# Five feed-forward parts on one core: a fourth pair of chunks as seven block products, all third and fourth block sums by accumulating transfers, and a new order of the units

## What is computed

```python
def swiglu(h, w_in, w_out):
    gate, up = jnp.split(h @ w_in, 2, axis=-1)
    return (jax.nn.silu(gate) * up) @ w_out      # first network: h 256 x 1024, hidden width 2816

def _swiglu(x, wg, wu, wd):                      # second network, four times
    return (jax.nn.silu(x @ wg) * (x @ wu)) @ wd

h = _swiglu(_rmsnorm(x, g[0]), ffn_w_gate[l, 0], ffn_w_up[l, 0], ffn_w_down[l, 0])
x = x + 0.5 * _rmsnorm(h, g[1])
```

## Time and profile before

| | before |
|---|---|
| median of three runs | 1266.3 us (1266.28 to 1269.35) |
| the profiled execution, its own time | 1265.96 us |
| its span, first to last instruction | 1264.2 us |
| TensorE busy | 1246.7 us (99%) |
| VectorE busy | 986.2 us (78%) |
| ScalarE busy | 757.5 us (60%) |
| GpSimd busy | 103.3 us (8%) |
| granted TensorE clock, mean | 0.999 |

### The profile page before, as it was taken

One profiled execution on the slowest core, in us unless ns is written; L12 is line 12 of the kernel. 1 busy time (PEld: TensorE's weight loads), 2 busy tenths in 40 slices (PEclk: granted clock), 3 DMA queues, 4 the chain that ended last, 5 costly groups with the idle time before them and its releaser, 6 DMA issues. The chain is left out here.

```text
span 1264.2 us, 16581 instructions
## 1 busy us (share of the span) xinstructions
PE 1246.7 (99%) x6615; PEld 1021.0 (81%) x6615; DVE 986.2 (78%) x1005; ACT 757.5 (60%) x929; POOL 103.3 (8%) x133
## 2 busy tenths in 40 slices
PE   8999999999999999999999999999999999999998
PEld 6887788887788888877888887888888897788886
DVE  4487788997898896676877986977976687888895
ACT  5344556565655665657665667565767555755663
POOL 3000000000554000100000000000000200000000
PEclk9999999999999999999999999999999999999999
DMA  9997499774598555662797565986763543598562
GB/s 335 370 401 248 136 351 282 265 208 157 169 327 283 200 150 200 204 182 69 268 292 236 171 183 165 338 261 183 214 209 109 184 137 131 196 306 263 200 176 75
DMA packets 150098, 279.23 MB, mean 221 GB/s; under 512 B 9800, under 2 KB 82820, under 8 KB 146820
## 3 DMA queue, kind: packets, MB, share of 16 engines
q1 hardware_dynamic: 143360, 243.28, 56.0%
q0 software_dynamic: 6288, 34.69, 12.0%
q10 hardware_dynamic: 372, 0.19, 0.1%
HBM read 248.73 MB, written 1.05 MB: 198 GB/s over the span
## 5 line engine op out<-in xcount | busy, mean ns | idle before, releaser
L2048 DVE TENSOR_TENSOR w_lo<-raw,w_hi 128x2048 fp32r<-128x2048 f32 x135 | 309.6, 2300 | 74.0 <-ACT w_hi L1476 73.6
L1476 ACT ACTIVATE w_hi<-raw 128x2048 fp32r<-128x2048 f32 x135 | 257.3, 1910 | 39.6 <-PE ps L740 26.9
L844 PE MATMUL ps<-w_hi,xT_pair 128*128 128x512 f32 x320 | 126.6, 396 | 0.0
L845 PE MATMUL ps<-w_hi,xT_pair 128*128 128x512 f32 x320 | 124.8, 390 | 0.0
L2048 DVE TENSOR_TENSOR w_lo<-arena,w_hi 128x2048 fp32r<-128x2048 f32 x45 | 102.9, 2286 | 12.7 <-ACT w_hi L1618 12.7
L738 PE MATMUL ps<-xT_pair,w_hi 128*128 128x256 f32 x368 | 107.6, 292 | 0.2 <-DVE xT_pair L2411 0.2
L739 PE MATMUL ps<-xT_pair,w_hi 128*128 128x256 f32 x368 | 104.0, 283 | 0.0
L740 PE MATMUL ps<-xT_pair,w_lo 128*128 128x256 f32 x368 | 104.0, 283 | 0.0
L1618 ACT ACTIVATE w_hi<-arena 128x2048 fp32r<-128x2048 f32 x45 | 86.1, 1913 | 24.8 <-PE ps L904 16.2
L904 PE MATMUL ps<-w_lo,hT_hi 128*128 128x512 f32 x360 | 97.5, 393 | 0.5
L904 PE MATMUL ps<-w_hi,hT_hi 128*128 128x512 f32 x360 | 96.8, 391 | 0.0
(11 more groups left out here) (327 smaller groups left out, 2636.8 us busy)
## 6 DMA issues: line engine op xcount, KB each, us to landing
raw<-in_ffn_w_down SPq DMA_DIRECT2D x88, 512.0 KB, 4.5
arena<-in_ffn_w_up SPq DMA_DIRECT2D x48, 512.0 KB, 5.4
raw<-in_ffn_w_gate SPq DMA_DIRECT2D x40, 512.0 KB, 4.0
raw<-in_ffn_w_up SPq DMA_DIRECT2D x40, 512.0 KB, 5.1
arena<-arena POOLq DMA_DIRECT2D x15, 1024.0 KB, 8.7
raw<-in_conv_w_in SPq DMA_DIRECT2D x24, 512.0 KB, 9.4
arena<-in_ffn_w_gate SPq DMA_DIRECT2D x24, 512.0 KB, 7.0
rows<-in_ffn_w_gate SPq DMA_DIRECT2D x24, 512.0 KB, 5.3
```

The source lines that it names most:

```text
L844: pe.matmul(ps[:, banks[t], :], xT_hi[:, 4 * h + k, tok(t)], hi[:, c], start=h == 0 and k == 0, stop=False, skip_group_check=True)
L845: pe.matmul(ps[:, banks[t], :], xT_lo[:, 4 * h + k, tok(t)], hi[:, c], start=False, stop=False, skip_group_check=True)
L1476: act.activation(w_hi[:, slot_of(n), :], raw[:, raw_slot(n), :], ACT.Copy).then_inc(hi_ready, 1)
L2048: dve.tensor_tensor(w_lo[:, slot_of(n), :], source(n), w_hi[:, slot_of(n), :].bitcast(F32), ALU.subtract).then_inc(raw_done, 1)
```

## The change

A fourth pair is added: chunks 2 and 3, 4 and 5, 6 and 7, 8 and 9 go in pairs, and only chunks 0, 1 and 10 by rows. A part has 45 units, not 42. All pairs take T3 and T4 by accumulating DMAs (`VECTOR_SUMS` holds T1 and T2 alone), T4 always in `b_21`. Pairs follow each other directly: the last product of pair p (T4) is unit 12, 21, 30 or 39, and B11 and B21 of the next pair are the two units behind it. Down units of a pair's two chunks come inside the next pair. GpSimd takes over one addition (`s_5` + `u_3`) and one multiplication (`u_2` by `s_1`) per pair, ScalarE the rescaling `final_x` of FFN1 and the distances of the AB mixer's bias (eight copies in FFN1). VectorE makes the tokens' sums `x_sums` earlier, right behind the first chunk. Signs are moved into the copies (scale -1), so the two products of `pair_hidden` become plain ones. In the diff the first loop over pairs is ScalarE's, the second VectorE's, and the last lines are GpSimd's `add_blocks`.

```diff
-SEVEN_UNITS = 42
+SEVEN_UNITS = 45
...
-QUAD_AT = ({8: Q_B21, 9: Q_B11, 10: Q_T1, 11: Q_T2, 13: Q_T3, 14: Q_B22, 15: Q_T4},
-           {19: Q_B21, 21: Q_B11, 22: Q_T1, 23: Q_T2, 25: Q_T3, 26: Q_B22, 27: Q_T4},
-           {28: Q_B21, 29: Q_B11, 31: Q_T1, 32: Q_T2, 34: Q_T3, 35: Q_B22, 36: Q_T4})
+QUAD_AT = ({5: Q_B11, 6: Q_B21, 8: Q_T1, 9: Q_T2, 10: Q_B22, 11: Q_T3, 12: Q_T4},
+           {13: Q_B11, 14: Q_B21, 16: Q_T1, 17: Q_T2, 19: Q_T3, 20: Q_B22, 21: Q_T4},
+           {22: Q_B11, 23: Q_B21, 25: Q_T1, 26: Q_T2, 28: Q_T3, 29: Q_B22, 30: Q_T4},
+           {31: Q_B11, 32: Q_B21, 34: Q_T1, 35: Q_T2, 37: Q_T3, 38: Q_B22, 39: Q_T4})
-QUAD_CHUNK = (3, 6, 8)
-ROW_CHUNKS = (0, 1, 2, 5, 10)
-VECTOR_SUMS = ((0, Q_T1), (0, Q_T2), (1, Q_T1), (1, Q_T2), (1, Q_T4), (2, Q_T1), (2, Q_T2))
+QUAD_CHUNK = (2, 4, 6, 8)
+QUAD_BANKS = ((0, 1, 3, 2), (2, 3, 0, 1), (1, 0, 2, 3), (3, 2, 1, 0))
+ROW_CHUNKS = (0, 1, 10)
+VECTOR_SUMS = tuple((p, q) for p in range(QUADS) for q in (Q_T1, Q_T2))
...
+                def next_block(i, p):
+                    u = UNIT_OF[p - 1]
+                    if i == 0:
+                        sp.wait_ge(sum_ok, sum_count(s, p - 1, Q_T1))
+                    for q in ((Q_B11,), (Q_T3,), (Q_B22, Q_T3), (Q_T4,))[i]:
+                        sp.wait_ge(raw_done, n + u[q] + 1)
+                    block(i, p)
...
+                next_block(1, 2)
+                next_block(2, 2)
+                next_block(3, 2)
+                next_block(0, 3)
...
+                def fill(p):
+                    def part(i, bank):
+                        c, u = QUAD_CHUNK[p - 1], UNIT_OF[p]
+                        if i == 0:
+                            pe.wait_ge(quad_hid, pair_no(s, p - 1) + 1)
+                            pe.wait_ge(quad_hid_first, pair_no(s, p - 1) + 1)
+                            turn_pair(QUAD_BANKS[p - 1][1], 0)
+                        if i == 1:
+                            down(u[Q_B21] + 1, c)
+                            turn_pair(QUAD_BANKS[p - 1][1], 1)
+                        if i == 2:
+                            down(u[Q_T2] + 1, c + 1)
+                    return part
...
+                for p in range(1, QUADS):
+                    u, turn, chunk = UNIT_OF[p], QUAD_BANKS[p - 1][1], QUAD_CHUNK[p - 1]
+                    hi(u[Q_B21] + 1)
+                    turned(chunk, turn)
+                    copies(p, Q_B11)
+                    hi(u[Q_T1])
+                    if s == FFN1 and p == 1:
+                        distances(0, SWA_HQ // 2)
+                    hi(u[Q_T2])
+                    turned(chunk + 1, turn)
+                    hi(u[Q_T2] + 1)
...
+                    copies(p, Q_T1)
+                    silu_first(p)
+                    hi(u[Q_T3])
+                    copies(p, Q_T2)
+                    hi(u[Q_B22], u[Q_T4])
+                    copies(p, Q_T3)
+                    hi(u[Q_T4] + 1, u[Q_T4] + 2)
+                    silu_second(p)
...
+                for p in range(1, QUADS):
+                    u, turn, chunk = UNIT_OF[p], QUAD_BANKS[p - 1][1], QUAD_CHUNK[p - 1]
+                    turned(chunk, turn)
+                    lo(u[Q_B21] + 1)
+                    sum_first(p)
+                    sum_second(p)
+                    lo(u[Q_T1])
+                    turned(chunk + 1, turn)
+                    lo(u[Q_T2])
+                    c_11(p)
+                    gate2_add(*((), (0, 1), (2, 3, 4), (5,))[p])
+                    lo(u[Q_T2] + 1, u[Q_T3], u[Q_B22])
+                    c_12(p)
+                    lo(u[Q_T4], u[Q_T4] + 1)
+                    pair_hidden(p)
+                    lo(u[Q_T4] + 2)
...
+                    pool.wait_ge(sum_ok, sum_count(s, p, Q_T2))
+                    pool.wait_ge(raw_done, n + u[Q_B21] + 1)
+                    pool.dma_start(b_21, t_2, accum_op=ALU.add).then_inc(t4_landed, 16)
+                    pool.wait_ge(quad_out, 6 * i + 5)
+                    pool.tensor_tensor(s_5, s_5, u_3, ALU.add).then_inc(c_second, 1)
+                    pool.wait_ge(c_ok, c_count(s, p, 1))
+                    pool.tensor_tensor(u_2, u_2, s_1, ALU.mult).then_inc(quad_hid_first, 1)
```

More of the change, by code:

```diff
@@ L30 @@
 NEG = -1e30
+FAR = 1e33
 SLOT = 2048
@@ L358, in block_program @@
         up_tok0 = sem("up_tok0")
-        quad_landed = [sem(f"quad_landed{i}") for i in range(3)]
+        quad_landed = [sem(f"quad_landed{i}") for i in range(4)]
         e_ok = sem("e_ok")
```

474 lines of the change are left out of this document (196 added, 278 removed).

## The result

The changed kernel takes **1443.8 us** (median; 1440.3 to 1444.7), the kernel before 1267.6 beside it: a ratio of 1.139 (95% interval 1.137 to 1.140). I had forecast 1409 with a range of 1355 to 1440. The direction and the mechanism held; the loss is 35 us larger, 3.8 us beyond the range.

What follows compares the result with a forecast made beforehand. TensorE bounds the kernel: 1266.0 us, less 13.6 (saved matmuls) and 4.5 (old waits), plus 144.0 (new waits, 28.8 in each of five parts), 9 (FFN0), 3 (FFN1) and 5 (clock), gives 1408.9, say 1409; range 1355 to 1440.

Steps and rivals of the forecast that it cites:

- What bounds the kernel before: TensorE, busy for 1246.7 of 1264.2 us, is the bound; whatever makes it wait is paid in full.
- The first handover at 5.5, the later ones at 5.1: Between pairs, B21's reload waits for T4's split: TensorE waits 5.5 us at the first handover, 5.1 at two more per part.
- R: Moment when VectorE has split T4 and B21's load may be issued; TensorE wants B21 at 4.1 us after it.
- T4's split behind `c_12`, 1.2: T4's split stands behind `c_12`, which waits for B22's product: 1.2 us of wait in each of three pairs.
- VectorE's list, 2.1 per later pair: From B21's start, VectorE's splits and sums come late for TensorE: waits of 0.8, 0.3 and 1.0, 2.1 us per later pair.
- Unit 7, 3.2: First pair's down unit: late split, then `sum_second` ahead of the `hT_lo` it needs; 3.2 us in sum per part.
- FFN0 ... together 9: Six `gate2_add` ahead of the second down unit's split, 7.7 us, and GpSimd's loads ahead of T4's transfer, 1.3.
- FFN1, 3: Four distance copies on ScalarE push T2's split by 1.6 us, `final_x` the first splits by some 1.4: 3.
- GpSimd's new addition and product ... cost nothing: GpSimd's two operations have 3 to 5 us each before anyone waits; the added T3 and T4 transfers also cost nothing.
- The pair at 39.1: Sign that the forecast is right: the period of a pair near 39.1 us in place of 30.8.
- The clock, 5: TensorE's clock falls in some of fifteen handover gaps and B21 runs at half rate: 0 to 9 us in all, 5 taken.
- stays low for long: Rival: B21 and the down unit behind it both run at half rate after each gap, 1495 us; chance 0.08.

Runs made afterwards that it cites:

- reload_in_before: Kernel before, with the third pair's B21 loaded only after VectorE has split T4 of the second pair: 1301.6 us, ratio 1.027.
- late_c12: Changed kernel, with T4's split ahead of `c_12` in the last three pairs: 1429.0 us, ratio 1.127 to the kernel before.
- warm: Changed kernel, with 22 dummy matmuls on TensorE ahead of the turn at each handover: 1444.8 us, ratio 1.141 to the kernel before.
- turn_first: Changed kernel, with the second `hT_lo` ahead of the block sum in the first pair: 1431.8 us, ratio 1.130 to the kernel before.
- gate_gap: Changed kernel, with FFN0's six `gate2_add` moved from ahead of the second down unit's split into the handover: 1434.0 us, ratio 1.132 to the kernel before.
- final_x_back: Changed kernel, with FFN1's `final_x` on VectorE again, not on ScalarE: 1441.1 us, ratio 1.137 to the kernel before.
- pool_off: Changed kernel, with GpSimd's new addition and product back on VectorE: 1439.7 us, ratio 1.138 to the kernel before.
- reload_first: Changed kernel, with SyncE issuing the load of the next B21 ahead of those of B12 and B22: 1427.1 us, ratio 1.127 to the kernel before.

## Why the prediction was right, and where its size failed

- **What bounds the kernel before: right.** Waits are paid in full there as soon as they appear, and so is the slower product behind them; reload_in_before adds no work and costs 34 us.
- **The first handover at 5.5, the later ones at 5.1: right in mechanism, near in size.** Expected: SyncE's load within 0.1 us of the split (0.03), B21 at R + 9.15 (R + 9.13), the later landings 5.2 us behind R (5.1 to 6.4), the first 7.0 behind it (7.5 to 8.1). What TensorE had to do behind R was taken 0.9 too short, so the later turns wait 3.8 to 5.2 us and not 5.1. Removing nine handovers gave 5.6 each. Of the 6.9 each for the five new ones in the old order 4.4 are wait, and most of the rest is the slow product.
- **T4's split behind `c_12`, 1.2: right as a wait** (1.43, of which a part is the stretched split). As a price it was wrong in kind: late_c12 removes it, and outside FFN0 0.3 to 2.1 us per part come back, for three such waits, since the reload's landing gives the pace.
- **VectorE's list, 2.1 per later pair: right as a chain, in part without effect.** Counted from B21's start (789.52), the second down unit's split ends at + 16.92 (forecast 17.0). But TensorE waits only 0.54 us for it in that pair, because B21 at the lower clock uses up time that it would have waited. With the clock held up (warm) it waits 0.59 and 0.69 at the two down units. No run took this term off by itself.
- **Unit 7, 3.2: right in kind.** TensorE waited 1.6 us per part for the `hT_lo` there, and turn_first takes most of that away. More came back than that, but half of it ahead of FFN0 and in FFN3, for which no cause is known. The other half of the term was not tried by itself.
- **"FFN0 ... together 9": wrong, this step failed most.** FFN0 grew by 18.6 us more than FFN2 (48.6 against 30.0). The step counted 6 x 1.28 and 1.3; it did not ask when the rows that `gate2_add` waits for would land. One wait of 5.16 on VectorE became 9.06 on TensorE. gate_gap brings 15.6 back in FFN0 in the profiled execution, and 9.8 in the time by the medians.
- **FFN1, 3: too low.** It grew by 34.5, 4.5 more than FFN2. final_x_back doesn't explain it; open.
- **"GpSimd's new addition and product ... cost nothing", and the same for the accumulating transfers: wrong as steps, small as prices.** The splits beside GpSimd take 3.20 and 3.37 us in place of 2.29, yet pool_off gives back only 4 us. The transfers land later than in the earlier trace rows; what that costs was not tried:

```profile
arena<-arena POOLq DMA_DIRECT2D x20, 1024.0 KB, 11.9
rows<-xn POOLq DMA_DIRECT2D x20, 1024.0 KB, 14.2
```

- **The pair at 39.1: too short.** The turns of FFN2's second, third and fourth pair start 40.96 and 40.24 us apart (the middle one at 788.75, shown above):

```profile
747.79 0.47 PE L884 MATMUL ps<-ident,arena 128*128 128x128 f32 x1 [5.64 <-DVE rows L2312]
...
828.99 0.33 PE L884 MATMUL ps<-ident,arena 128*128 128x128 f32 x1 [3.88 <-DVE rows L2312]
```

  For the first of the two I can name 0.9 (the stretched split of T4) and 0.44 (TensorE's restart at T4, behind a copy out of PSUM on ScalarE). But pool_off shows that taking the 0.9 away does not return it, so this is a reading of one timeline and not a shown cause.
- **The clock, 5: right that it falls; no cost was found.** The row went to 0.58 behind the gap; warm undid that and gained nothing. The forecast's argument, that VectorE's chain lets TensorE lose some of it for nothing, held for all of it as far as these runs tell. Its rival "stays low for long" falls too: the mean over the whole run is 0.961.
- **Sum of the misses.** By the forecast's terms, with 1 us of clock for each part, the parts should have taken 221.8, 211.5, 206.7, 206.7 and 199.1. They took 13.4, 5.3, 3.8, 7.2 and 4.3 more, 34.0 together, of 34.9. FFN0 is the largest and its cause is shown by gate_gap, its size only to between 10 and 16 us. In the others 4 us each is what GpSimd's operations and restarts could be; that is not shown. Of FFN3's further 3.4 over FFN2, the same code, 1.9 are two reloads: its later ones landed 5.7 and 6.4 us behind R, FFN2's both 5.1. Why they did is open, and in turn_first and reload_first the two parts are of one length within 0.5 us.

The range failed for the same reason: its upper end took in slower reloads and the clock, each of the two on the reload's chain. It held nothing for VectorE waiting on a transfer in FFN0, or for engines that hold each other up.

## What to carry to other kernels

When an edit lets a buffer be built in place by one step and loaded again for the next, count the distance between its last reader and its next reader, and compare it with landing plus copy plus all that stands behind the copy in its engine's list; here TensorE had 5.0 us of other work and 9.1 were needed, fifteen times, against 13.6 us of matmuls saved. An operation that is moved onto the critical list brings its own wait along: charge not only how long it runs but when its input lands. And before a later piece of a chain is shortened, ask what has it pinned: where a reload sets the pace, an earlier request can take longer to land, as in pool_off and late_c12.
